# Routing chain of a routed mixture layer: one maximum over five sets, rounding for comparison tables, source rows before destination rows

## What is computed

```python
lg = (t @ w_rg) + b_rg                      # 4 group logits of a token
g_idx = argmax(lg);  g_w = softmax(lg)[g_idx]
le_sel = ((t @ w_re) + b_re).reshape(-1, 4, 4)[g_idx]   # 4 expert logits of the chosen group
top_v, top_i = top_k(le_sel, 2)
top_w = softmax(top_v) * g_w
# out = sum over a token's two experts e of  top_w * ((silu(t @ w_gate[e]) * (t @ w_up[e])) @ w_down[e])
```

## Time and profile before

| | us |
|---|---|
| runs | 647.06 median of 3 (645.36 to 649.06) |
| the profiled execution | 648.02 |
| its span in the trace | 646.2 |
| PE busy in the span | 589.2 (91%) |
| DVE busy | 212.9 (33%) |
| ACT busy | 199.3 (31%) |
| POOL busy | 51.5 (8%) |
| HBM traffic | 141.63 MB read, 9.45 MB written |

### The profile page before, as it was taken

The page is one execution under the profiler, slowest core; times in us unless marked ns, Lnnn a source line. Parts: engine busy times, 40 slices in busy tenths (PEclk is TensorE's granted clock), DMA queues, the critical chain, the costliest instruction groups (busy, mean ns, idle before and its releaser), DMA issues.

```text
span 646.2 us, 9470 instructions
## 1 busy us (share of the span) xinstructions
PE 589.2 (91%) x3456; PEld 382.4 (59%) x3457; DVE 212.9 (33%) x475; ACT 199.3 (31%) x434; POOL 51.5 (8%) x91
## 2 busy tenths in 40 slices
PE   6999999999999999999678999999999987926994
PEld 6998877878989999974222333333333332304883
DVE  3621264565444343277000111101111010064653
ACT  5532354555543543342100001001010010062774
POOL 0000000000000000000201121121221211110000
PEclk9899999999999999989797999999999999986998
DMA  9743123203210249836696499999999999934001
GB/s 317 199 172 131 65 66 131 65 8 125 66 66 1 66 166 420 354 139 256 245 422 246 183 421 420 421 421 421 421 422 421 422 418 421 410 115 182 33 33 65
DMA packets 47216, 151.52 MB, mean 234 GB/s; under 512 B 7880, under 2 KB 27216, under 8 KB 34640
## 3 DMA queue, kind: packets, MB, share of 16 engines
q1 hardware_dynamic: 43504, 139.77, 55.2%
q0 software_dynamic: 3392, 11.02, 4.4%
q10 hardware_dynamic: 288, 0.29, 0.2%
HBM read 141.63 MB, written 9.45 MB: 234 GB/s over the span
## 4 chain that ended last, share of the span: by engine, by line
PE 79%; DMA 7%; DVE 6%; issue 3%; SPq 2%; ACT 2%; DVEq 0%; POOLq 0%; POOL 0%; ACTq 0%
PE bank L1598 19%; PE bank L1320 13%; PE bank L1321 12%; PE bank L1322 12%; PE bank L1624 10%; DMA ring_dn<-in_w_down 5%; PE bank L1402 2%; SPq L585 2%; PE bank L1584 2%; PE bank L1375 2%; DVE ple_lo L1253 2%; DMA gmix<-in_norm_mix 1%; PE bank L1527 1%; PE bank L1610 1%; PE bank L1416 1%
## 5 line engine op out<-in xcount | busy, mean ns | idle before, releaser
L1598 PE MATMUL bank<-ring_gu,rowsT 128*64 128x512 f32 (+1 forms) x800 | 147.0, 608 | 6.6 <-issue 3.0
L1598 PEld LDWEIGHTS bank<-ring_gu,rowsT 128*64 128x64 f32 (+1 forms) x800 | 44.2, 129 | 94.5 <-issue 90.3
L1624 PE MATMUL bank<-ring_dn,hidT 128*64 128x512 f32 (+1 forms) x400 | 75.8, 606 | 7.0 <-DMA ring_dn<-in_w_down 3.7
L880 ACT ACTIVATE silu_g<-bank 128x256 f32<-128x256 f32 x20 | 7.7, 383 | 224.0 <-PE bank L1598 224.0
L1069 DVE TENSOR_TENSOR w_lo<-w_raw,w_hi 128x2048 fp32r<-128x2048 f32 x18 | 41.3, 2292 | 76.9 <-ACT w_hi L745 69.6
L1219 DVE TENSOR_TENSOR hid<-silu_g,bank 128x256 f32<-128x256 f32 x20 | 8.4, 421 | 153.4 <-ACT silu_g L880 153.4
L1320 PE MATMUL bank<-w_hi,hT_hi 128*128 128x256 f32 x192 | 56.1, 292 | 0.9 <-issue 0.9
L1321 PE MATMUL bank<-w_lo,hT_hi 128*128 128x256 f32 x192 | 54.9, 286 | 0.0
L1322 PE MATMUL bank<-w_hi,hT_lo 128*128 128x256 f32 x192 | 54.9, 286 | 0.0
L1320 PE MATMUL bank<-hT_hi,w_hi 128*128 128x512 f32 x128 | 50.8, 397 | 0.0
L1321 PE MATMUL bank<-hT_lo,w_hi 128*128 128x512 f32 x128 | 49.9, 390 | 0.0
(11 more groups left out here) (214 smaller groups left out, 902.0 us busy)
## 6 DMA issues: line engine op xcount, KB each, us to landing
ring_gu<-in_w_gate SPq DMA_DIRECT2D x32, 1024.0 KB
ring_gu<-in_w_up SPq DMA_DIRECT2D x32, 1024.0 KB
ring_dn<-in_w_down SPq DMA_DIRECT2D x16, 2048.0 KB, 21.3
w_raw<-in_w_in SPq DMA_DIRECT2D x14, 1024.0 KB, 5.0
w_raw<-in_w_out SPq DMA_DIRECT2D x4, 1024.0 KB, 4.9
ple_gate_raw<-in_w_ple_gate SPq DMA_DIRECT2D x1, 4096.0 KB, 28.9
yg<-y_rows SPq DMA_DIRECT2D x8, 512.0 KB, 7.4
xr<-in_x SPq DMA_DIRECT2D x4, 512.0 KB, 9.1
```

Of the source, the lines that this page charges most:

```text
L1598: last = T.matmul(b_gu[q * BLK + t:q * BLK + t + n, :], rowsT[:, k % 4, k // 4, t:t + n], ring_gu[s][:, :, k, q * UC:(q + 1) * UC], start= ...
L1624: last = T.matmul(b_dn[q * BLK + t:q * BLK + t + n, :], hidT[:, kf % 2, kf // 2, t:t + n], ring_dn[s][:, kf, q * (D // 2):(q + 1) * (D // 2)],
```

## The change

1. `first_max` takes any number of sets. The first call goes over all five sets of four of every tile (the group logits and the four groups' expert logits, 128x80) and the second over the four expert sets with each one's first choice masked (128x64). The picking of the chosen group's logits is gone; the group's one-hot is multiplied in afterwards. `prefix` is made with two additions (pairs of tiles, then pairs of pairs) instead of four. Five memsets stand ahead of the wait for the logits. The two inputs of ScalarE's exponentials are computed behind `member_ready`.
2. Counts are rounded up to multiples of 32, and slots down to blocks of 64, by adding and subtracting a large constant instead of comparing with tables. Slots of both choices are made in one multiplication.
3. `blk_rows` is made in two halves, sources before destinations, and TensorE makes the rows in two passes of 8 matmuls of 28 columns, sources into `b_rank`, destinations into `b_o`. VectorE writes `src_row` first, as int32 and without a copy, and signals `rows_ready`; destinations follow, and `grp_ge` and `grp_e` stand behind the source rows.
4. TensorE's order becomes: product 0, rank matmuls, products 1 and 2, source rows, destination rows, products 3 to 7.
5. POOL's first two gathers take their row numbers straight from columns of `src_row` and stand ahead of the reading of the number of blocks.

The core of the diff:

```diff
-                first_max(lg[:, :, 0:N_GROUPS], gmax, oh_g)
-                V.tensor_tensor(gsub[:], ...).then_inc(gsub_ready, 1)
-                link(V.tensor_tensor(picked[:], lg[:, :, N_GROUPS:NR]..., wide(oh_g[:], 4), ALU.mult))
-                link(V.tensor_reduce(les[:], picked[:].rearrange("p t g j -> p t j g"), X, ALU.add))
-                first_max(les[:], v_top[0], oh[0])
-                link(V.scalar_tensor_tensor(les2[:], oh[0][:], MASKED, les[:], ALU.mult, ALU.add))
-                first_max(les2[:], v_top[1], oh[1])
-                V.tensor_tensor(vd[:], v_top[1][:], v_top[0][:], ALU.subtract).then_inc(vd_ready, 1)
+                first_max(lg[:].rearrange("p t (g j) -> p (t g) j", j=4), best[0], oh[0])
+                link(V.scalar_tensor_tensor(les2[:]..., top1..., MASKED, lg[:, :, N_GROUPS:NR], ALU.mult, ALU.add))
+                first_max(les2[:].rearrange("p t g j -> p (t g) j"), best[1], oh[1])
+                V.tensor_tensor(E[:, 0], top1, wide(in_group, 4), ALU.mult)
+                link(V.tensor_tensor(E[:, 1], oh[1][:], wide(in_group, 4), ALU.mult))
+                link(V.tensor_tensor(member[:, 1:], Ef[:, 0], Ef[:, 1], ALU.add))
+                link(V.tensor_tensor(with_last[:, 2:], member[:, 1:], member[:, 0:NT], ALU.add))
+                V.tensor_tensor(prefix[:, 1:], with_last[:, 2:], with_last[:, 0:NT], ALU.add).then_inc(member_ready, 1)
...
                 dve.wait_ge(rank_done, 1)
-                link(V.tensor_copy(counts[:], ...))
-                link(V.tensor_tensor(nb_gt[:], wide(counts[:], GPE), ..., ALU.is_gt))
-                link(V.tensor_reduce(nb[:], nb_gt[:], X, ALU.add))
-                link(V.tensor_scalar(nb1[:], nb[:], 1.0, None, ALU.max))
+                link(V.tensor_scalar(nb_r[:], b_rank[:, NT * 16:NT * 16 + 16], GRP / 2 - 0.5, ROUND_GRP, ALU.add, ALU.add))
+                link(V.tensor_scalar(nb[:, 1:], nb_r[:], -ROUND_GRP, float(GRP), ALU.add, ALU.max))
...
-                link(V.tensor_tensor(past_edge[:], wide(pairs, TABLE), all_pairs(edges), ALU.is_ge))
-                link(V.tensor_reduce(blk_f[:], past_edge[:], X, ALU.add))
+                link(V.tensor_scalar(blk_r[:], pairs, 0.5 - BLK / 2, ROUND_BLK, ALU.add, ALU.add))
+                V.scalar_tensor_tensor(in_blk[:], blk_r[:], -ROUND_BLK, pairs, ALU.add, ALU.subtract)
+                link(V.tensor_tensor(blk_oh[:], wide(blk_r[:], TABLE), all_pairs(blk_marks), ALU.is_equal))
+                rows_in_blocks(0)
+                V.tensor_tensor(slot_oh[:], wide(in_blk[:], P), all_pairs(minus_slot), ALU.is_equal).then_inc(slot_oh_ready, 1)
+                rows_in_blocks(1).then_inc(slot_oh_ready, 1)
...
+                V.tensor_tensor(src_row[:], b_rows[0], row_offset[:, 0:TABLE], ALU.add).then_inc(rows_ready, 1)
...
+                dve.wait_ge(rows_done, 2)
+                V.tensor_tensor(dst_row[:], b_rows[1], row_offset[:, TABLE:], ALU.add).then_inc(rows_ready, 1)
```

On TensorE and POOL:

```diff
-            for n in range(3):
-                ple_product(n)
+            ple_product(0)
             pe.wait_ge(member_ready, 1)
...
-            for n in range(3, 7):
+            for n in range(1, 3):
                 ple_product(n)
-            pe.wait_ge(slot_oh_ready, 1)
-            for n in range(2 * NT):
-                last = T.matmul(b_rank[:, P:P + 2 * TABLE], slot_oh[:, n, :], blk_rows[:, n]..., ...)
-            last.then_inc(rows_done, 1)
-            ple_product(7)
+            for w in range(2):
+                pe.wait_ge(slot_oh_ready, 1 + w)
+                for n in range(2 * NT):
+                    last = T.matmul(b_rows[w], slot_oh[:, n, :], blk_rows[:, w, n, :], ...)
+                last.then_inc(rows_done, 1)
+            for n in range(3, 2 * NT):
+                ple_product(n)
...
-            total = pool.value_load(cum_i[0:1, N_EXPERTS - 1:N_EXPERTS], ...)
             for b in range(ROW_BUFS):
-                gather(b, b, b, b + 1)
+                gather(b, bass.IndirectOffsetOnAxis(ap=src_row[:, b:b + 1].bitcast(U32), axis=0))
+            pool.wait_ge(rows_ready, 2)
+            total = pool.value_load(cum_i[0:1, N_EXPERTS - 1:N_EXPERTS], ...)
```

More of the change, by code:

```diff
@@ L61 @@
 TABLE = MAX_BLOCKS + 3
[L62 removed]
+SMALL = 2 * P + 4 + 64 + TABLE + 5 + P + 16 + 2 * TABLE
 HALF = D // 2
@@ L76 @@
 ROUND = 1.5 * 2.0 ** 23
+ROUND_GRP = ROUND * GRP
+ROUND_BLK = ROUND * BLK
 RING = 3
@@ L352, in trunk @@
         lg = routing("lg", [P, NT, NR])
[L353 to L357, removed]
+        best = [routing(f"best{k}", [P, NT, n]) for k, n in enumerate((5, 4))]
+        eq = routing("eq", [P, NT * 5, 4])
+        cand = routing("cand", [P, NT * 5, 4])
+        cmin = routing("cmin", [P, NT * 5])
+        oh = [routing(f"oh{k}", [P, NT, n, 4]) for k, n in enumerate((5, 4))]
+        les2 = routing("les2", [P, NT, 4, 4])
         gsub = routing("gsub", [P, NT, 4])
@@ L361, in trunk @@
         g_w = routing("g_w", [P, NT])
[L362 to L366, removed]
+        vgap = routing("vgap", [P, NT, 4])
+        vpick = routing("vpick", [P, NT, 4])
         vd = routing("vd", [P, NT])
@@ L673, in column, with gather @@
                 return bass.IndirectOffsetOnAxis(ap=now[:].bitcast(U32), axis=0)
-            def gather(b, buf, now, n_columns):
-                rows_of = column(src_now[now], src_row, b)
-                pool.wait_ge(column_ready, n_columns)
+            def gather(buf, rows_of):
                 pool.sem_inc(gathers_begun, 1)
@@ L681, in gather, with gather_by_column @@
                                         in_offset=rows_of).then_inc(s_rows[buf], 16)
+            def gather_by_column(b, buf, now, n_columns):
+                rows_of = column(src_now[now], src_row, b)
+                pool.wait_ge(column_ready, n_columns)
+                gather(buf, rows_of)
             def scatter(b, buf, n_columns):
@@ L991, in route @@
-                Ef = E[:].rearrange("p k t g j -> p k t (g j)")
-                link(V.tensor_tensor(member[:], Ef[:, 0], Ef[:, 1], ALU.add))
-                link(V.memset(prefix[:, 0, :], 0.0))
-                for i in range(NT):
-                    link(V.tensor_tensor(prefix[:, i + 1, :], prefix[:, i, :], member[:, i, :], ALU.add))
-                V.memset(one16[:], 1.0).then_inc(member_ready, 1)
-                dve.wait_ge(rank_done, 1)
-                link(V.tensor_copy(counts[:], b_rank[:, NT * 16:NT * 16 + 16]))
@@ L1008, in route @@
+                link(V.tensor_tensor_scan(cum[:], one17[:], nb[:], 0.0, ALU.mult, ALU.add))
                 link(V.tensor_tensor(slots[:], b_rank[:, 0:NT * 16].rearrange("p (t e) -> p t e", t=NT),
-                                     first32[:].unsqueeze(1).to_broadcast([P, NT, 16]), ALU.add))
-                for k in range(TOP_K):
-                    link(V.tensor_tensor(slot_e[:, k], Ef[:, k], slots[:], ALU.mult))
+                                     all_tiles(cum[:, 0:N_EXPERTS]), ALU.add))
```

129 lines of the change are left out of this document (62 added, 67 removed).

## The result

The changed kernel takes 644.53 us (median of 9 runs, 642.57 to 647.14); the kernel before, run beside it, 648.82 (9 runs, 645.36 to 650.99). The ratio is 0.9943, with a 95% interval of 0.992 to 0.9965: a gain of about 0.6%, some 3.7 us. The profiled execution took 644.17 us, its span is 642.3 us, 3.9 less than before.

The account below looks back on a forecast made before the run. The weight stream bounds the kernel, its end pinned to TensorE's first four blocks. Block 0 starting 2.45 us earlier plus 2.0 from its clock, 4.45, less 1.7 for half clock, leaves 2.75 from 647.06: 644.3 us, range 641.3 to 647.3.

Parts of the forecast that it names:

- Maxima and ranks: VectorE membership ready at 290.9 instead of 292.5; after the rank matmuls VectorE goes on at 292.05, 3.9 us earlier.
- Rounding: VectorE chain from ranks to row tables: 3.8 us instead of 6.2, ready at 295.8, meeting TensorE's products 1 and 2.
- Row passes: TensorE's two 28-column row passes: 1.8 us each, paced by weight loads, so 1.8 us more work than before.
- The gather: POOL's first gather lands at 302.3 instead of 310.7; 8 us on paper, not collected because products 3 to 7 follow.
- The clock: Light rank and row matmuls on TensorE: a late rise at 292 or fall at 297 to 301 likely, costing 1.7 us.
- The case forecast: One half-clock stretch on TensorE: 4.45 - 1.7 = 2.75 us gained, 644.3 us; chance 0.42.
- Block 0's clock: Block 0's first matmuls take 7.05 instead of 9.07 us, as TensorE is never idle long ahead of it; 2.0 us.
- If those come X us earlier, the load at 363.40 does too, and all behind it: X is worth X: TensorE's first four blocks pin the SP load at 363.40 and the stream's end, so their gain passes on in full.
- the lucky end of its range: First blocks: one of their stalls or half-clock stretches gone would give 1.5 us more; low end of the range.
- The rival in which the first blocks eat the gain: First blocks: one more instruction stall and a half-clock stretch take 3.9 of the 4.45 us; 646.5 to 647.1; chance 0.10.
- The end as much earlier: Sign at the kernel's end: load at 363.40 moves to 359 to 361, and the end by the same amount.

Follow-up runs that it names:

- one_pass: The changed kernel with the rows made in one pass of 8 matmuls of 56 columns instead of two passes; 643.55 us, ratio 0.9921.
- old_gather: The changed kernel with POOL's old way to the first gathers (wait for both tables, read number of blocks, copy column); 645.13 us, ratio 0.9945.
- product_between: The changed kernel with product 3 set between the source and destination row passes; 643.28 us, ratio 0.9916.
- pe_order_only: The kernel before with TensorE's order alone changed to the new one; 645.66 us, ratio 0.9964.
- old_pe_order: The changed kernel with products 0 to 2 ahead of the ranks, 3 to 6 ahead of both row passes, 7 behind; 646.58 us, ratio 0.9967.
- delay: The changed kernel with product 7's matmuls made three times, adding 3.4 us ahead of block 0 and 16 instructions; 644.59 us, ratio 0.9948.
- after_again: The changed kernel run once more, unchanged, to see what repeats; 645.24 us, ratio 0.994.
- early_transpose: The changed kernel with block 0's rows transposed and moved between products 5 and 6; 642.22 us, ratio 0.9908.
- one_pass_early_hold: The changed kernel with one row pass, transposes ahead of products 6 and 7, and expert 3's reload held; 638.41 us, ratio 0.9854.
- less_warm: The changed kernel with 16 warming matmuls at the start instead of 24, 32 instructions fewer; 646.98 us, ratio 0.9987.
- hold: The changed kernel with the SP queue holding expert 3's reload until half of block 1's gate and up matmuls are done; 643.27 us, ratio 0.9929.
- one_pass_early: The changed kernel with one row pass and transposes ahead of products 6 and 7; 641.85 us, ratio 0.9909.
- after: The changed kernel itself, against the kernel before; 644.53 us, ratio 0.9943.

## Why the prediction came out as it did

The time (644.3 forecast, 644.53 measured) is closer than its working deserves. One step failed, and another gave it back. The starting point was off too: the forecast took 2.75 us from 647.06, the median of three, and beside the changed kernel the kernel before took 648.82. The medians differ by 4.3 us (3.7 by the ratio, 2.3 to 5.2), so an error of 1.5 us in the gain and one of 1.8 in the starting point nearly cancelled.

**Maxima and ranks: right.** Membership was ready at 290.38 (290.9); the five memsets overlap (285.57 to 285.67, 0.1 and not 0.4). Ranks ran in 291.24 to 292.19, VectorE went on at 292.23 (292.05).

**Rounding: right.** slot_oh and TensorE's rows met at 296.08 (295.8).

**Row passes: right,** and the most instructive term. At 28 columns a pass costs about as much as at 56 columns (1.7 to 2.0 us, and 1.9 to 2.0), because loads of weights set the pace: PEld is busy 3.10 of 3.10 us. One_pass confirms that the second was for nothing.

**The gather: right.** It was issued at 299.28 and landed 3.5 us later, and the rows wait for TensorE until 310; old_gather shows that its time is hidden.

**The clock: right.** The fall came at 299.3, in the second pass, for 3.5 us; products 3 to 7 took 10.04 instead of the 8.66 of one_pass. The case forecast had 310.3 + 1.7 = 312.0 for block 0, measured 311.99. One_pass and product_between remove the cause and the effect goes.

**Block 0's clock: right.** 7.1 us in every run with the new order, pe_order_only among them; 9.5 in old_pe_order. TensorE's matmul side was 2.73 us earlier at the end of these matmuls; 2.75 was the sum.

**"If those come X us earlier, the load at 363.40 does too, and all behind it: X is worth X": wrong.** This is the step that failed. It treats the way from block 0 to the load, and from there to the end, as rigid. 2.73 at block 0 came with 6.1 at the load. As far as block 2 the step nearly held (3.12); what it put at nothing is the clock of block 2's matmuls, 10.06 us before and 7.09 after, which is 3.0 of the excess of 3.4. The prediction had this only as the lucky end of its range, one stretch gone, at 1.5. In the experiments the same term goes the other way: one_pass's block 0 is 3.4 us earlier than the changed kernel's, its block 2 2.6, its load only 1.1, for 1.5 went to half clock in block 2. And in delay the first blocks took up 1.9 us of 3.3 by themselves. The rival in which the first blocks eat the gain named the right place; in this pair they added to it instead. That TensorE stands there for instruction fetches, the prediction had read rightly. The Trainium skill's "Advanced Engine Details and Errata" (ISA Cache) says that code is cached in lines of 16 KB; the fetches here are of that size. What a fetch costs beside a full stream, these traces alone show.

**"The end as much earlier": wrong as well,** by 2.2 us. The load moved by 6.1 and the end by 3.9, since the last awaited down product ran at half clock behind a wait for its weights (5.35 instead of 3.65). Why the clock fell there and not before is not settled. In one_pass, product_between and after_again there are such stretches of 3.4 us near the end too; in early_transpose, one_pass_early_hold and the kernel before there are none between 500 and 560 us.

The two errors, 3.4 too much at the load and 2.2 lost at the end, cancelled in large part: the spans differ by 3.9 where 2.75 was forecast.

**What stays open.** Differences under about 2 us between two of these kernels are within their intervals. Single executions scatter with the clock of the whole program: of the 25 of the kernel before in the second session, the one of 642.66 us had a mean granted clock of 0.964, that of 651.56 us 0.952. What part of the 3.7 us is luck of the clock, in block 2 and near the end, can't be told from this; each new program length places its stalls anew, and less_warm suggests that this alone can weigh 2.5 us. That TensorE stands for fetches is concluded from the nearly fixed distance and from hold; that they are late because of the weight loads rests on hold and one_pass_early_hold alone. One fetch came 3.1 us behind the last beside a full stream too (delay's third; the changed kernel's fifth, 3.8 behind, came as its stream ran out at 340.2), so the queueing itself was not seen.

## What to carry to other kernels

Before you count a gain at the start of a stage as a gain at its end, look at what lies in between that needn't move with it, above all stretches at half clock and waits for code. A run that adds a known delay asks for this directly, but it moves the code as well: compare the start of each later stage in it, and not only the end, with several other runs. Where a program branches into code for the first time, try keeping the DMA queues free for that stretch if the transfer has slack later (here the median fell by 3.4 us from one_pass_early, with intervals that overlap a little, and by 1.3 from the changed kernel, which isn't clear of noise). Making a matmul narrower saves nothing once weight loads set its pace, and two narrow passes in a row can cost the clock besides: put dense work between them, or make one pass.

## What the runs showed of the hardware that was not expected

- Instruction fetches of 16 KB mostly started 5.4 to 7.1 us apart beside a weight stream of 405 to 424 GB/s, and 3.0 to 3.8 where it was held (hold's second and third, the first three of one_pass_early_hold). One branch lasted 4.1 us in the changed kernel and 6.1 in the kernel before, up to 2.5 us after a fetch had started.
- Two passes of light matmuls together, 3.5 to 4.5 us with PE busy throughout, brought a granted clock of 0.50 for 3.4 us or more, beginning in the second pass or at most 0.6 us behind it, in every run that had them ahead of the products (after, after_again, delay, old_gather, hold, early_transpose, less_warm) and in old_pe_order; single passes of 1.7 to 2.0 us never did. PE was busy throughout, so here its busy time didn't tell whether the clock would stay.
- 32 instructions fewer at the start of the program moved a stall 330 us later from one instruction to another, and the median was about 2.5 us higher.
- Five memsets in a row on VectorE started 0.01 to 0.04 us apart, at 0.06 to 0.09 each.
